# Attention with the values stationary, output transposed, and the output projection's weights loaded in the attention stage

## The reference

```
q = rope(q) * scale ; k = rope(k)          # latent rows; context rows without rope
s_loc = where(|i - j| <= 128, q k^T, -inf) # latent query against latent keys
s_ctx = q kc^T                             # against the context keys
p = softmax([s_loc, s_ctx, sink])[..., :-1]  # one sink logit per head, dropped after
o = p[..., :span] v + p[..., span:] vc
y = o @ w_o                                # (tokens, 1024) @ (1024, 1024)
```

## Time and profile before

| | us |
|---|---|
| three runs | 2038.61, 2043.62, 2047.23 |
| median | 2043.62 |
| profiled execution, its own time | 2040.56 |
| its span, first to last instruction | 2038.7 |
| TensorE busy in the span | 1738.8 (85%) |
| VectorE / ScalarE busy | 769.4 / 432.5 |
| attention stage | 152.7 to 271.8 |
| projection "ao" | 272.1 to about 356 |

### The profile page before, as it was taken

The page is one execution under the profiler, slowest core; times in us unless marked ns, Lnnn a source line. Parts: engine busy times, 40 slices in busy tenths (PEclk is TensorE's granted clock), DMA queues, the critical chain, the costliest instruction groups (busy, mean ns, idle before and its releaser), DMA issues. The chain is left out here.

```text
span 2038.7 us, 33252 instructions
## 1 busy us (share of the span) xinstructions
PE 1738.8 (85%) x11224; PEld 1095.9 (54%) x11225; DVE 769.4 (38%) x1683; ACT 432.5 (21%) x801; POOL 270.6 (13%) x322
## 2 busy tenths in 40 slices
PE   4989989769999999999994699847669999999996
PEld 2768854536666666665661486213445555555553
DVE  3425633352222222212222763681434344333444
ACT  3214421001111111111110245660101111111111
POOL 2020010001111111111110340220011111111110
PEclk8999989779999999999997799978779999999998
DMA  9750052259999999999956553513749999999993
GB/s 343 252 187 1 1 190 107 107 228 374 414 418 415 415 415 406 400 396 390 395 207 275 194 129 117 186 62 155 284 191 420 419 419 415 416 415 416 416 415 123
DMA packets 122426, 587.67 MB, mean 288 GB/s; under 512 B 25690, under 2 KB 46800, under 8 KB 61184
## 3 DMA queue, kind: packets, MB, share of 16 engines
q1 hardware_dynamic: 96160, 510.18, 62.8%
q0 software_dynamic: 25920, 73.71, 9.8%
q10 hardware_dynamic: 288, 3.01, 0.4%
HBM read 584.65 MB, written 28.39 MB: 301 GB/s over the span
## 5 line engine op out<-in xcount | busy, mean ns | idle before, releaser
L1698 PE MATMUL ps<-m_wgu,m_xT 128*64 128x256 f32 x2944 | 330.8, 381 | 8.9 <-DMA m_wgu<-in_moe_w_up 7.3
L1698 PEld LDWEIGHTS ps<-m_wgu,m_xT 128*64 128x64 f32 x2944 | 253.1, 138 | 96.9 <-issue 37.9
L1956 PE MATMUL ps<-m_wgu,m_xT 128*64 128x256 f32 x2112 | 250.9, 385 | 4.3 <-DVE m_xT L2055 4.3
L1956 PEld LDWEIGHTS ps<-m_wgu,m_xT 128*64 128x64 f32 x2112 | 158.5, 138 | 98.6 <-issue 47.0
L1728 PE MATMUL ps<-mods,m_hidT 128*64 128x512 f32 x736 | 169.8, 602 | 31.6 <-ACT m_hidT L1750 20.3
L1792 DVE SCALAR_TENSOR_TENSOR m_hid<-m_act_g,m_meta,ps 128x256 f32<-128x256 f32 x46 | 22.1, 480 | 329.5 <-ACT m_act_g L1747 329.5
L2061 DVE TENSOR_TENSOR h<-h,ps 128x512 f32<-128x512 f32 x132 | 90.6, 686 | 124.2 <-PE ps L1945 123.2
L1989 PE MATMUL ps<-m_wd,m_hidT 128*64 128x512 f32 x528 | 120.6, 597 | 6.2 <-DMA m_wd<-in_moe_w_down 5.0
L1728 PEld LDWEIGHTS ps<-mods,m_hidT 128*64 128x64 f32 x736 | 58.5, 137 | 111.1 <-issue 111.1
L1896 POOL MEMSET h<- 128x1024 f32 x35 | 33.3, 953 | 522.9 <-PE ps L1934 405.5
L1642 POOL DMA_INDIRECT h<-h_rows,m_gidx x49 | 50.1, 1023 | 371.1 <-DVE m_gidx L1781 366.9
(11 more groups left out here) (428 smaller groups left out, 2816.2 us busy)
## 6 DMA issues: line engine op xcount, KB each, us to landing
m_wgu<-in_moe_w_gate SPq DMA_DIRECT2D x135, 1024.0 KB
m_wgu<-in_moe_w_up SPq DMA_DIRECT2D x135, 1024.0 KB, 11.7
mods<-in_moe_w_down SPq DMA_DIRECT2D x69, 1024.0 KB, 17.2
m_wd<-in_moe_w_down SPq DMA_DIRECT2D x66, 1024.0 KB, 8.6
c_rows<-y_rows SPq DMA_DIRECT2D x8, 2048.0 KB, 16.3
mods<-in_ada_w SPq DMA_DIRECT2D x14, 1024.0 KB, 5.0
mods<-in_ada_w POOLq DMA_DIRECT2D x11, 1024.0 KB, 5.3
mods<-in_lru_w_in SPq DMA_DIRECT2D x10, 1024.0 KB, 7.3
```

What stands on the lines that cost most here:

```text
L1698: last = pe.matmul(g.ps[half[s], GU, a * FE:(a + 1) * FE], xT[:, k, half[s]], wgu[:, bufs[s][0], bufs[s][1], a, k, :], start=(k == 0), sto ...
L1956: last = pe.matmul(g.ps[half[s], GU, a * FE:(a + 1) * FE], xT[:, k, half[s]], wgu[:, q, s, a, k, :], start=(k == 0), stop=(k == KD - 1))
```

## The change

Three things are done.

1. The roles in the multiplication with the values are exchanged. The values of one key/value head (128x64) are stationary, and the turned probabilities of its four query heads move at once, 512 columns. Two such heads fill the two halves of the output's partitions. So `mix` is called once per eight units instead of once per unit, for the eight heads together; all eight turned blocks must be kept, in two sets of eight (one in a new tile, one in `g.h`, which is free in this stage).
2. The output comes with heads on the partitions and tokens along the row, `oT`, as the projection needs it. The turning of `o` at the start of "ao" goes. But the reciprocal row sums now vary along the row and have to be spread over the partitions: TensorE turns them (8x128), VectorE copies them (`shareT`), TensorE multiplies them with a 0/1 matrix `pick`, ScalarE copies the 128x512 result into `oT`, and VectorE multiplies the output with it.
3. `w_o` is loaded by SP at the start of the attention stage, in eight transfers of 64 partitions (the order of its rows follows that of `oT`). In "lo" the load stays where it was.

```diff
-    T_BANK, O_BANK = 4, 6
+    T_BANK, O_BANK, R_BANK = 4, 6, 7
+    RING = 2 * HALF                       # HALF = 8, GROUPS_OF = 8
-        probT = sb("probT", [P, 2, TOK])
+        probT = [sb("probT", [P, HALF, TOK])[:], g.h[:].rearrange("p t (u c) -> p (t u) c", c=TOK)]
+        pick = sb("pick", [HALF, GROUP, P])
+        shareT = sb("shareT", [HALF, P])
 # SP
                 sp.dma_start(sink[:], ...)
+                weights.load(sp)
 # TensorE
-                def mix(u):
...
-                        last = pe.matmul(g.ps[:, O_BANK + hd // HALF, (hd % HALF) * HD:(hd % HALF + 1) * HD],
-                                         probT[:, u % 2, j * P:(j + 1) * P], v[:, j, kvh * HD:(kvh + 1) * HD],
+                def mix(n):
+                    t, jp = divmod(n, 2)
+                    pe.wait_ge(evac_v, HALF // 2 * (n + 1))
+                    pe.wait_ge(evac_a, HALF // 2 * (n + 1))
+                    if n:
+                        pe.wait_ge(o_evac, n)
+                    for j in range(j0, TILES):
+                        for s in range(2):
+                            kvh = 2 * jp + s
+                            last = pe.matmul(g.ps[HD * s:HD * s + HD, O_BANK, :]..., v[:, j, kvh * HD:(kvh + 1) * HD],
+                                             probT[n % 2][:, s::2, j * P:(j + 1) * P], start=(j == j0), stop=(j == TILES - 1))
+                def turn_shares(n):
+                    pe.wait_ge(share_s, n + 1)
+                    if n:
+                        pe.wait_ge(spread_out, n)
+                    pe.transpose(g.ps[0:HALF, R_BANK, 0:P], rowsum[:, t, hs], g.ident).then_inc(share_turned, 1)
+                def spread_shares(n):
+                    pe.wait_ge(shareT_s, n + 1)
+                    for h in range(GROUP):
+                        last = pe.matmul(g.ps[:, R_BANK, h * P:(h + 1) * P], pick[:, h, :], shareT[:], start=True, stop=True)
...
                     turn(u)
-                    if u:
-                        mix(u - 1)
+                    n = u // HALF - 1
+                    if n >= 0 and u % HALF == 2:
+                        mix(n)
+                    if n >= 0 and u % HALF == 5:
+                        turn_shares(n)
+                    if n >= 0 and u % HALF == 7:
+                        spread_shares(n)
+                mix(GROUPS_OF - 1)
+                turn_shares(GROUPS_OF - 1)
+                spread_shares(GROUPS_OF - 1)
 # VectorE, step u, n = u // 8 - 1
+                def scaled_out(n):
+                    dve.wait_ge(mixed, n + 1)
+                    dve.wait_ge(spread_out, n + 1)
+                    dve.tensor_tensor(out, g.ps[:, O_BANK, :]..., out, ALU.mult).then_inc(o_evac, 1)
-                    if u % HALF == 4 and u >= HALF and u < len(units):
-                        finish(u // HALF - 1)
-                finish(len(units) // HALF - 1)
+                    if u % HALF == 0:
+                        sink_args(n)
+                        if n:
+                            scaled_out(n - 1)
+                    if u % HALF == 4:
+                        shares(n)
+                    if u % HALF == 6:
+                        shares_out(n)
+                n = GROUPS_OF - 1
+                sink_args(n)
+                scaled_out(n - 1)
+                shares(n)
+                shares_out(n)
+                scaled_out(n)
 # ScalarE
+                def share_rows(n):
+                    act.wait_ge(spread, n + 1)
+                    act.activation(oT[...], g.ps[:, R_BANK, :]..., ACT.Copy).then_inc(spread_out, 1)
+                    if u % HALF == 0 and n:
+                        share_rows(n - 1)
+                    if u % HALF == 2:
+                        sink_terms(n)
 # project_phase
-                if src is not None:
-                    for t in range(tiles):
...
-                            last = pe.transpose(g.ps[:, k // 4, (k % 4) * P:(k % 4 + 1) * P], src[:, t, k::KD], g.ident)
...
-                        act.activation(srcT[:, 0:KD // 2, t * P:(t + 1) * P], ...)
...
-                        dve.tensor_copy(srcT[:, KD // 2:KD, t * P:(t + 1) * P], ...)
-                for i in range(nk // WG):
-                    sp.dma_start(w[0:kp, WG * i:WG * (i + 1), :], w_dram[:, WG * i:WG * (i + 1), :])
+                if not spare:
+                    weights.load(sp)
```

More of the change, by code:

```diff
@@ L742, in _, with __init__, load, wait @@
                         copy(u - LAG)
-                    if u % HALF == 4 and u >= HALF and u < len(units):
-                        sink_terms(u // HALF - 1)
-                sink_terms(len(units) // HALF - 1)
-def project_phase(g, tag, w_dram, kp, nk, tiles, srcT=None, src=None, spare=None):
-    rows = kp if srcT is None else srcT.shape[0]
+                    if u < HALF or u >= len(units):
+                        continue
+                    n = u // HALF - 1
+                    if u % HALF == 0 and n:
+                        share_rows(n - 1)
+                    if u % HALF == 2:
+                        sink_terms(n)
+                sink_terms(GROUPS_OF - 1)
+                share_rows(GROUPS_OF - 2)
+                share_rows(GROUPS_OF - 1)
+class ProjectWeights:
+    WG = 2
+    def __init__(self, g, sb, tag, nk, rows):
+        self.w = sb(tag + "_w", [P, nk, D])
+        self.rows, self.steps = rows, nk // self.WG
+        self.ready = [g.sem(f"{tag}_w_ready{i}") for i in range(self.steps)]
+    def load(self, sp):
+        for i in range(self.steps):
+            for part, source in self.rows(self.WG * i, self.WG * (i + 1)):
+                sp.dma_start(self.w[part, self.WG * i:self.WG * (i + 1), :], source).then_inc(self.ready[i], 16)
+    def wait(self, pe, k):
+        pe.wait_ge(self.ready[k // self.WG], 16 * len(self.rows(0, self.WG)))
+def project_phase(g, tag, weights, nk, tiles, srcT, spare=None):
     nc = g.nc
@@ L758, in project_phase @@
         sb = lambda n, s, d=F32: st.enter_context(nc.sbuf_tensor(n, s, d))
[L759 to L763 removed]
+        w = weights.w
+        gated = sb(tag + "_gated", [P, 2, D])
         late_mods = MOD_LOADS1[2:] if g.mod_layer else []
         mod_in = g.sem(tag + "_mod_in")
[L767 to L768 removed]
+        done, h_stored = g.sem(tag + "_done"), g.sem(tag + "_h_stored")
         hturned, hT_done = g.sem(tag + "_hturned"), g.sem(tag + "_hT_done")
@@ L782, in project_phase @@
         with nc.Block() as block:
-            def pad(eng, first):
-                for i in range(first, nk // WG, 2):
-                    eng.memset(w[64:rows, WG * i:WG * (i + 1), :], 0.0).then_inc(padded[first], 1)
             @block.gpsimd
             def _(pool):
-                if rows > kp:
-                    pad(pool, 1)
                 if ada:
@@ L833, in _ @@
                     for k in range(nk):
-                        if t == 0 and k % WG == 0:
-                            pe.wait_ge(w_ready[k // WG], 16)
+                        if t == 0 and k % weights.WG == 0:
+                            weights.wait(pe, k)
                         for j in range(2):
@@ L873, in _ @@
             def _(dve):
-                if src is not None:
-                    for t in range(tiles):
-                        dve.wait_ge(turned, t + 1)
-                        dve.tensor_copy(srcT[:, KD // 2:KD, t * P:(t + 1) * P],
-                                        g.ps[:, 1, :].rearrange("p (k c) -> p k c", c=P)).then_inc(turned_v, 1)
-                if rows > kp:
-                    pad(dve, 0)
                 if late_mods:
```

95 lines of the change are left out of this document (44 added, 51 removed).

## The result

The changed kernel took 2047.52 us (median of 20 runs, 2041.55 to 2054.5); the kernel before took 2043.64 (20 runs). The ratio is 1.002, with a 95% interval of 1.0012 to 1.0029: slower by 0.2%, where 0.5% faster was forecast. The profiled execution has a span of 2045.8 us and a mean clock of 0.925 (before 2038.7 and 0.934). The forecast of 2033.8 was 13.7 us too low, and the time lies above its range.

A forecast was written before the change was run, and what follows sets the result against it. TensorE was taken to bound the latent half, a VectorE-ScalarE chain the context half. Projection's start -10.0 and attention's end +0.2 gave -9.8 us: 2033.8 against the median of 2043.62, range 2024 to 2044.

The forecast's parts named there:

- the third rival: Attention's context half: clock falls, sets take 16.8 us in place of 10.8, +24, in sum 2058 us; chance 0.05.
- the walk's turn at 2.80 us: Context unit: TensorE's turn comes 2.80 us after spreading ends, with work for 1.1, leaving a hole of 1.7 us.
- chain (b): Behind L678 VectorE copies 8x128 ahead of a maximum: turn 2.0 us after L678, TensorE having 1.1 to 2 of work.
- The first rival: Attention stage: copies, semaphores and engine order cost 1 us more in each of seven sets, +7, 2040.8 us; chance 0.15.
- The start: Start of the attention stage: as before, with unit 2 beginning at 160.25 since unit 0 has no multiplication.
- The projection's start: Start of the projection: 32 transposes, eight copies and their waits go, 10.0 us won, all on the path.
- The halves at once: Multiplication with the values: two half-width passes run at once, 3.42 us per latent set, 1.71 per context set.
- full drain: Changing TensorE's tiling mode: would cost some 0.55 us per set, 4.4 in all, against the 2 counted.
- The tail: End of attention: last multiplication at half clock, spreading at full, 9.0 us; bounds 6.9 to 9.9.
- That the stage's end and not its length decides: Stages after attention and the projection's start: they start when these end, so they only shift.
- some 8 us of the 10 would come back: Projection's weights left at its start: they would hold up the first tile, returning 8 us of the gain.

The follow-up runs named there:

- first filler: Changed kernel with six bf16 multiplications of 512 columns ahead of the turns of units 1 and 7 in each context set, behind the copy's wait; 2052.21 us, ratio 1.0044.
- copy first: Changed kernel with ScalarE's copy of turned unit u-2 put ahead of its exponential of unit u; 2037.24 us, ratio 0.9969.
- spaced: Changed kernel with the same instructions, each step of the reciprocals' way given one or more units of slack; 2029.87 us, ratio 0.9932.
- Filling the holes: Changed kernel with twelve and six matmuls of 256 columns ahead of the scores that precede turns 1 and 7 of each context set; 2043.56 us, ratio 0.9994.
- The late load: Changed kernel with the projection's weights loaded at the start of the projection stage, as before the change; 2072.9 us, ratio 1.0145.

## Why the prediction was wrong

**The failed step is the argument against the third rival** (the clock falls inside the context half), "scores run in every unit, and 35 busy of 40 kept 1.00; I expect 4 x 8.4 of 4 x 10.8, 34 of 43". I had only set one busy share beside another, and given the rival 0.05. The two were not even alike, 0.88 before and 0.79 expected, and the trace of before has no stretch at 1.00 between them. So it excluded nothing, and the rival deserved more than one chance in twenty. Context sets of the runs, each from one spreading to the next (before: between two waits of L660):

| kernel, set | TensorE idle before a turn | busy | clock |
|---|---|---|---|
| before, 235.82 to 246.16 | 1.25 (before L660) | 9.09 of 10.34 | 1.00 |
| changed, 237.47 to 249.09 | 1.74, 0.82 | 9.05 of 11.62 | 1.00, falls 2 us later |
| first filler, 253.31 to 267.31 | 1.65, 0.74 | 11.61 of 14.00 | 1.00 |
| copy first, 233.23 to 244.25 | 1.38, 0.46 | 9.18 of 11.02 | 1.00 |
| spaced, 231.64 to 241.77 | 0.59, 0.48 | 9.06 of 10.13 | 1.00 |

The changed kernel's set has the lowest share as well as the longest hole. The runs don't separate the two, and the first filler's set shows that holes of that length can stand at 1.00. The rival's price was off as well: the clock came back each time, so the whole half did not run at 0.50. Filling the holes gave back 5.3 us of stage time, and the fall that it left costs about 1 more (48.8 us against 4 x 11.6 + 1.25 = 47.7); I had priced 24. The Trainium skill ("TensorE: Matmul & The Clock Gate", section on the PE-mode transpose) has it that transposes don't count as busy in the same way as other passes, which spoke for this rival; the outcome goes the same way, but no run here takes the turns out, so their part in it isn't shown.

**The second failed step is the walk's turn at 2.80 us**, which had no term for a copy queued on ScalarE. It came 3.09 after the end of spreading (238.55 to 241.64). The exponential was as walked; ScalarE's copy of unit u-2 stands behind it, on the same bank. The same 0.3 came in chain (b), so a full-clock set is 11.6 where I had 10.8; putting the copy first took 0.6 of that away. Of the other 0.2, the multiplication has 0.1 (the turn ahead of it ends its pace at 242.54, the scores behind it run at theirs from 244.61: 2.07 us for my 1.96), and 0.1 stays unexplained. In the latent half the holes are 1.13 and 0.21 where I had 0.75 and none, and copy first took 2.5 of the 2.9 us there. So longer holes account for some 6 us and the clock for some 6, the latter as a consequence of idle time. The first rival (holes 1 us larger in each of seven sets, +7) and the third one, at a quarter of its price, came together, a case that the forecast had no chance for.

**The start.** Of the 1.7 us the stage before gives 1.0 (this stage began at 153.74, before at 152.74), and 0.7 is a clock that rises later in the first units. Over the runs here the first turn lies between 158.36 and 160.14, with and without the early transfers, and I count it as spread between executions.

**What held.** The projection's start: no transposes, a first pass 0.33 us behind the end of L737, no wait for `ao_w`. The halves at once: 16 passes in 3.59 us (174.81 to 178.40 in the changed kernel), against the 3.42 at my pace; the scores behind them take 0.1 longer than others, in sum 0.27 where I had counted 0.25. The Trainium skill ("TensorEngine Tiling (Array Packing)", Key Properties) states that changing the mode drains the engine; the 0.55 us per set that I had estimated for a full drain is not seen. The tail, 9.5 for 9.0, with the multiplication at half clock (3.68). That the stage's end and not its length decides: what follows shifted, with a difference of 4.8 us at the projection and 3.9 in the medians.

**Priced wrongly, off the path of the forecast.** The late load: "some 8 us of the 10 would come back" was 25. Of the 17 us beyond it, 12 to 13.5 are what the cut into halves of 64 partitions costs in the kernel before; the rest is open.

## What to carry to other kernels

Before trusting a walk over several engines, write down every semaphore the waiting instruction has and what is queued ahead of each producer; the one left out here cost 0.3 us a hole, and with it gone the clock stayed up in three of four sets. When a change adds a way over three engines, put a unit of other work between each producer and its consumer: the same instructions in another order were worth 18 us. A busy share at which the clock held is no evidence for a lower one, nor for another pattern of idle time; where TensorE's work shrinks and waits gather, give the fall of the clock a real chance.

## What the runs showed of the hardware

- The clock stayed at 1.00 in three sets of 11.0 us with idle holes of 1.38 and 0.46 us, and fell to 0.50 in 7 of 9 sets of the same work with holes of 1.74 and 0.82. In the changed kernel it fell while TensorE was busy, some 2 us behind a hole. A filler of bf16 passes into an unused part of a score bank held it up, for a net gain of 0.26% with more work.
- 4 MB in eight transfers of 64 partitions moved at about 200 GB/s, and in four transfers of 128 partitions, from the same queue, at 334 GB/s. With the DMA otherwise idle the last landed 17.8 us after its issue (changed kernel) and 12.1 (kernel before, loads moved forward); beside the modulation's weights it was 28.8 and 28.9 for the halves and 18.8 for whole ones. In a quiet stretch:

```profile
154.00:174.00 20.00, 20.00 (x109) 15.92 (x109) 14.52 (x33) 11.48 (x29) 0.00 (x0) 0.88 0.97 199
```

```profile
154.00:166.00 12.00, 12.00 (x64) 9.54 (x63) 6.61 (x15) 5.16 (x13) 0.00 (x0) 0.82 0.86 334
```

The first is the changed kernel (DMA share 0.97 at 199 GB/s), the second the kernel before with its loads moved forward (0.86 at 334): the engines are as busy, or more so, with 0.6 of the bytes in each us.
